# Latent-attention softmax scale folded into q's norm weight, shorter Newton steps, and a reordered start in a two-layer encoder trunk

## What is computed

```python
# rms_norm(x, gain) = x * rsqrt(mean(x*x) + 1e-6) * gain
a_q, a_k, a_v, b_ql, b_kvl, b_kr = split_cols(h @ w_in, (512, 512, 512, 256, 128, 32))
a_q = rope(rms_norm(a_q.reshape(B, S, 8, 64), a_q_norm), pos)          # a_k the same
out_a = differential_attention(..., A_QK_DIM ** -0.5)                  # 4 heads, two softmaxes each
q_b  = (rms_norm(b_ql,  b_q_a_norm)  @ b_w_q_b ).reshape(B, S, 8, 64 + 32)
kv_b = (rms_norm(b_kvl, b_kv_a_norm) @ b_w_kv_b).reshape(B, S, 8, 64 + 64)
q_nope = rms_norm(q_nope, b_q_nope_norm); k_nope = rms_norm(k_nope, b_k_nope_norm)
q_rope = rope(rms_norm(q_rope, b_q_rope_norm), pos); k_rope = rope(rms_norm(b_kr, b_k_rope_norm), pos)
# latent attention, 8 heads, per 128 queries, chunk-causal in chunks of 64 frames
s = (q_nope @ k_nope.T + q_rope @ k_rope.T) * (64 + 32) ** -0.5
p = softmax(where(mask, s, -inf)); out_b = p @ b_v
x = x + concat(out_a, out_b) @ w_out
```

## Time and profile before

| | |
|---|---|
| median of three runs | 1354.26 us |
| profiled run, its own time | 1355.07 us |
| its span | 1353.2 us |
| TensorE busy | 1284.9 us (95%), 6308 matmuls |
| VectorE busy | 617.3 us (46%), 1110 instructions |
| ScalarE busy | 559.3 us (41%), 921 instructions |
| GpSimd busy | 506.2 us (37%), 215 instructions |
| latent units | 89.8 to 211.4 us |
| differential heads | about 211 to 290 us |

### The profile page before, as it was taken

One profiled execution on the slowest core, in us unless ns is written; L12 is line 12 of the kernel. 1 busy time (PEld: TensorE's weight loads), 2 busy tenths in 40 slices (PEclk: granted clock), 3 DMA queues, 4 the chain that ended last, 5 costly groups with the idle time before them and its releaser, 6 DMA issues.

```text
span 1353.2 us, 16953 instructions
## 1 busy us (share of the span) xinstructions
PE 1284.9 (95%) x6308; PEld 1082.6 (80%) x6308; DVE 617.3 (46%) x1110; ACT 559.3 (41%) x921; POOL 506.2 (37%) x215
## 2 busy tenths in 40 slices
PE   8878888999999999999989999998999999999998
PEld 8777887877888888888868888887788888888887
DVE  6579986754222112222248888887332220122211
ACT  5534454654332212223346777775433322122320
POOL 4422311126444434445542222221654454344441
PEclk9888998999999999999989999999999999999999
DMA  5210100012323322233211111110222332222341
GB/s 193 67 63 31 48 32 31 32 41 81 109 93 117 102 78 93 93 105 107 84 64 62 46 46 46 51 57 31 79 94 93 100 118 93 78 93 93 111 131 39
DMA packets 29142, 105.83 MB, mean 78 GB/s; under 512 B 3360, under 2 KB 3616, under 8 KB 29088
## 3 DMA queue, kind: packets, MB, share of 16 engines
q1 hardware_dynamic: 28944, 105.07, 23.5%
q10 hardware_dynamic: 144, 0.02, 0.0%
HBM read 102.98 MB, written 2.10 MB: 78 GB/s over the span
## 4 chain that ended last, share of the span: by engine, by line
PE 68%; DVE 18%; ACT 8%; issue 4%; POOL 1%; DMA 0%; ACTq 0%; DVEq 0%; POOLq 0%
PE bank L338 19%; PE bank L342 19%; PE bank L339 19%; DVE cs_hi L1469 2%; DVE cs_lo L1471 1%; ACT ca L1427 1%; ACT w_hi L314 1%; ACT ca L1425 1%; DVE tiny L1044 1%; ACT cq_hi L1508 1%; DVE pn L1059 1%; PE bank L916 1%; PE bank L1011 1%; PE bank L918 1%; PE bank L920 1%
## 5 line engine op out<-in xcount | busy, mean ns | idle before, releaser
L326 POOL TENSOR_TENSOR w_lo<-wraw,w_hi 128x1024 fp32r<-128x1024 f32 (+4 forms) x180 | 458.3, 2547 | 781.2 <-ACT w_hi L314 781.1
L338 PE MATMUL bank<-h_hi,w_hi 128*128 128x512 f32 x896 | 353.5, 395 | 1.0 <-DVE h_lo L424 1.0
L339 PE MATMUL bank<-h_lo,w_hi 128*128 128x512 f32 x896 | 351.2, 392 | 0.0
L314 ACT ACTIVATE w_hi<-wraw 128x1024 fp32r<-128x1024 f32 (+4 forms) x180 | 197.2, 1096 | 156.7 <-DVE x L631 127.2
L342 PE MATMUL bank<-h_hi,w_lo 128*128 128x512 f32 x896 | 223.6, 392 | 0.0
L338 PEld LDWEIGHTS bank<-h_hi,w_hi 128*128 128x128 f32 x896 | 168.8, 188 | 38.5 <-DVE h_lo L424 1.7
L339 PEld LDWEIGHTS bank<-h_lo,w_hi 128*128 128x128 f32 x896 | 168.9, 189 | 36.2
L342 PEld LDWEIGHTS bank<-h_hi,w_lo 128*128 128x128 f32 x896 | 168.3, 188 | 36.8
L338 PE MATMUL bank<-f_hi,w_hi 128*128 128x512 f32 x352 | 137.7, 391 | 0.0
L339 PE MATMUL bank<-f_lo,w_hi 128*128 128x512 f32 x352 | 137.7, 391 | 0.0
L617 DVE TENSOR_TENSOR fu<-bank,rstd 128x512 f32<-128x512 f32 x44 | 30.4, 691 | 200.3 <-PE bank L342 200.3
(11 more groups left out here) (273 smaller groups left out, 2028.1 us busy)
## 6 DMA issues: line engine op xcount, KB each, us to landing
wraw<-in_w_in SPq DMA_DIRECT2D x120, 512.0 KB, 3.3
wraw<-in_w_down SPq DMA_DIRECT2D x32, 704.0 KB, 4.1
wraw<-in_w_ab SPq DMA_DIRECT2D x20, 512.0 KB, 3.2
x<-in_xt SPq DMA_DIRECT2D x8, 256.0 KB, 5.3
out<-x SPq DMA_DIRECT2D x8, 256.0 KB, 2.1
wraw<-in_w_ab SPq DMA_DIRECT2D x4, 416.0 KB, 5.3
wraw<-in_w_ab SPq DMA_DIRECT2D x2, 384.0 KB, 3.1
wraw<-in_w_ab SPq DMA_DIRECT2D x2, 256.0 KB, 2.8
```

The costliest lines, as they stand in the source:

```text
L314: nc.scalar.activation(whi[:, s, 0:width], wraw[:, s, 0:width], ACT.Copy).then_inc(S("w_hi"), 1)
L326: nc.gpsimd.tensor_tensor(wlo[:, s, 0:width], wraw[:, s, 0:width], whi[:, s, 0:width], ALU.subtract).then_inc(S("w_lo"), 1)
L338: nc.tensor.matmul(out_bank, w, src_hi[kt], start=(kt == 0), stop=False)
L339: nc.tensor.matmul(out_bank, w, src_lo[kt], start=False, stop=False)
```

## The change

It does six things.

- The latent score scale B_SCALE is multiplied into the weight of q's norm (`T_BQ`) once, so scores come scaled; the maximum is then taken negated (`negate=True`) straight into the bias column, L1046 goes, and the exp has scale 1. Newton q0 and q1 likewise give roots with A_SCALE in them, through their means (`T_EQ`), so the step after them (L980) goes.
- A Newton refinement has three instructions instead of four, two of them with a scalar and two tensors; `b_mean_dve` reads eps from a spread column instead of an immediate.
- The probabilities are scaled by a two-tensor multiply with the reciprocal as a spread column, instead of a tensor-scalar one.
- On ScalarE w_hi of chunks 4 and 5 stand ahead of lambda's exp and of the latents' root; GpSimd makes w_lo of chunk 4 before the table tbk. VectorE does lambda after the latents' scaling.
- TensorE's latent transposes stand between the two halves of the first projection. `b_pair(0)` on VectorE stands behind the k/v blocks of the second half.
- In a unit the third projection block stands ahead of the transposes of the probabilities, and all values stand at the end.

```diff
@@ -393,13 +396,11 @@
         dve.wait_ge(S("rs_exp"), r + 1)
-        nc.vector.tensor_tensor(a, m, y, ALU.mult).then_inc(S("rs_step"), 1)
-        dve.wait_ge(S("rs_step"), 3 * r + 1)
+        nc.vector.scalar_tensor_tensor(a, m, -0.5, y, ALU.mult, ALU.mult).then_inc(S("rs_step"), 1)
+        dve.wait_ge(S("rs_step"), 2 * r + 1)
         nc.vector.tensor_tensor(a, a, y, ALU.mult).then_inc(S("rs_step"), 1)
-        dve.wait_ge(S("rs_step"), 3 * r + 2)
-        nc.vector.tensor_scalar(a, a, -0.5, 1.5, ALU.mult, ALU.add).then_inc(S("rs_step"), 1)
-        dve.wait_ge(S("rs_step"), 3 * r + 3)
-        nc.vector.tensor_tensor(tiny[:, at:at + n], a, y, ALU.mult).then_inc(S("rs_root"), 1)
+        dve.wait_ge(S("rs_step"), 2 * r + 2)
+        nc.vector.scalar_tensor_tensor(tiny[:, at:at + n], a, 1.5, y, ALU.add, ALU.mult).then_inc(S("rs_root"), 1)
...
@@ -692,8 +695,9 @@
         dve.wait_ge(S("l_eps"), 1)
-        nc.vector.tensor_scalar(col(T_E, NB), col(T_M + 3 * NB, NB), EPS, None, ALU.mult).then_inc(S("l_eps"), 1)
-        dve.wait_ge(S("l_eps"), 2)
+        for t, scale in ((T_E, EPS), (T_EQ, EPS / A_SCALE ** 2)):
+            nc.vector.tensor_scalar(col(t, NB), col(T_M + 3 * NB, NB), scale, None, ALU.mult).then_inc(S("l_eps"), 1)
+        dve.wait_ge(S("l_eps"), 3)
         dve.wait_ge(S("l_sum"), NB)
...
@@ -857,9 +861,10 @@
         dve.wait_ge(S("bk_sum"), NB * hf + NB)
-        nc.vector.tensor_scalar(col(T_M, 32), col(T_BS + 48 * hf, 32), 1.0 / B_NOPE, EPS, ALU.mult, ALU.add)
-        nc.vector.tensor_scalar(col(T_M + 32, 16), col(T_BS + 48 * hf + 32, 16), 1.0 / B_ROPE, EPS, ALU.mult,
-                                ALU.add).then_inc(S("rs_mean"), 1)
+        nc.vector.scalar_tensor_tensor(col(T_M, 32), col(T_BS + 48 * hf, 32), 1.0 / B_NOPE, spread(col(T_EPS), [P, 32]),
+                                       ALU.mult, ALU.add)
+        nc.vector.scalar_tensor_tensor(col(T_M + 32, 16), col(T_BS + 48 * hf + 32, 16), 1.0 / B_ROPE,
+                                       spread(col(T_EPS), [P, 16]), ALU.mult, ALU.add).then_inc(S("rs_mean"), 1)
...
@@ -968,17 +973,11 @@
         dve.wait_ge(S("pj_sum"), 2 * p + 2)
-        e = spread(col(T_E, NB).rearrange("p (i o) -> p i o", o=1), [P, NB, 4])
+        e, n = ((T_EQ, A_DIM * A_SCALE ** 2), (T_E, A_DIM))[p // 2]
+        e = spread(col(e, NB).rearrange("p (i o) -> p i o", o=1), [P, NB, 4])
         nc.vector.scalar_tensor_tensor(col(T_M, 16).rearrange("p (i j) -> p i j", i=NB),
-                                       col(T_AS + 16 * p, 16).rearrange("p (i j) -> p i j", i=NB), 1.0 / A_DIM, e, ALU.mult,
+                                       col(T_AS + 16 * p, 16).rearrange("p (i j) -> p i j", i=NB), 1.0 / n, e, ALU.mult,
                                        ALU.add).then_inc(S("rs_mean"), 1)
-
-    def q_root_dve(dve, p):
-
-        rs_newton_dve(dve, GROUPS[p], 16, Z_Q + 16 * p)
-        dve.wait_ge(S("rs_root"), ROOT[GROUPS[p]] + 1)
-        nc.vector.tensor_scalar(col(Z_Q + 16 * p, 16), col(Z_Q + 16 * p, 16), A_SCALE, None,
-                                ALU.mult).then_inc(S("a_zq"), 1)
...
@@ -1041,13 +1038,11 @@
         o = bank[0][:].rearrange("p (b n) -> p b n", b=2) if c == 0 else b_score_of(b)
-        nc.vector.reduce_max(col(T_MX + b, n), o, AX).then_inc(S("h_mx"), 1)
-        dve.wait_ge(S("h_mx"), 3 * u + c + 1)
-        nc.vector.tensor_scalar(col(T_NM + b, n), col(T_MX + b, n), -B_SCALE, None, ALU.mult).then_inc(S("h_nm"), 1)
+        nc.vector.tensor_reduce(col(T_NM + b, n), o, AX, ALU.max, negate=True).then_inc(S("h_nm"), 1)
...
         act.wait_ge(S("h_nm"), 3 * u + max(b, 1))
-        nc.scalar.activation(p_of(pn, b), b_score_of(b), ACT.Exp, bias=col(T_NM + b), scale=B_SCALE,
+        nc.scalar.activation(p_of(pn, b), b_score_of(b), ACT.Exp, bias=col(T_NM + b), scale=1.0,
                              accum_out=col(T_L + b)).then_inc(S("h_e"), 1)
...
@@ -1056,7 +1051,8 @@
         for j in range(b, b + n):
-            nc.vector.tensor_scalar(p_of(pn, j), p_of(pn, j), col(T_R + j), None, ALU.mult).then_inc(S("h_p"), 1)
+            nc.vector.tensor_tensor(p_of(pn, j), p_of(pn, j), spread(col(T_R + j), [P, SW[j]]),
+                                    ALU.mult).then_inc(S("h_p"), 1)
...
@@ -1114,14 +1110,14 @@
         nc.scalar.activation(bqhi[0:B_QK, :], bank[TRQ][0:B_QK, :], ACT.Copy,
-                             scale=v(V_BQ, rows=B_QK)).then_inc(S("h_qhi"), 1)
+                             scale=tiny[0:B_QK, T_BQ:T_BQ + 1]).then_inc(S("h_qhi"), 1)
         act.wait_ge(S("h_kt"), u + 1)
...
         dve.wait_ge(S("h_qhi"), u + 1)
-        nc.vector.scalar_tensor_tensor(bqlo[0:B_QK, :], bank[TRQ][0:B_QK, :], v(V_BQ, rows=B_QK), bqhi[0:B_QK, :],
+        nc.vector.scalar_tensor_tensor(bqlo[0:B_QK, :], bank[TRQ][0:B_QK, :], tiny[0:B_QK, T_BQ:T_BQ + 1], bqhi[0:B_QK, :],
                                        ALU.mult, ALU.subtract).then_inc(S("h_qlo"), 1)
...
@@ -1620,12 +1616,11 @@
                                                [P, NB, n]), ALU.mult).then_inc(S("tabs"), 1)
-            for g in range(4):
+            for g in range(5):
                 lo(g)
...
             table(tbk, NB * 2 * A_DIM, 4 * A_DIM + 2 * B_ROPE, 2 * B_ROPE)
-            lo(4)
             lo(5)
...
@@ -1681,13 +1676,13 @@
                     hi_static(act, d // 2)
-            act.wait_ge(S("lam_sum"), 1)
-            nc.scalar.activation(tiny[:, T_LE:T_LE + 2], bank[5][:, 0:2], ACT.Exp).then_inc(S("lam_exp"), 1)
             hi_static(act, 4)
             for i in range(NB):
                 lat_sq_act(act, i)
+            hi_static(act, 5)
             rs_act(act, "lat", 16)
-            hi_static(act, 5)
+            act.wait_ge(S("lam_sum"), 1)
+            nc.scalar.activation(tiny[:, T_LE:T_LE + 2], bank[5][:, 0:2], ACT.Exp).then_inc(S("lam_exp"), 1)
             for i in range(NB):
                 lat_scale_act(act, i)
...
@@ -1840,17 +1835,24 @@
             nc.vector.memset(zeros[:, 0:SEQ].bitcast(F32), 0.0).then_inc(S("zeros"), 1)
+            nc.vector.memset(col(T_EPS), EPS)
             dve.wait_ge(S("vec_in"), 16)
...
                                     ALU.mult)
+            nc.vector.tensor_scalar(tiny[:, T_BQ:T_BQ + 1], v(V_BQ), B_SCALE, None, ALU.mult)
             for d in range(KT):
...
             nc.vector.tensor_copy(ident_r[:], M["ident"])
+            for i in range(NB):
+                lat_sum_dve(dve, i)
+            lat_mean_dve(dve)
+            rs_newton_dve(dve, "lat", 16, Z_LAT)
+            lat_scale_dve(dve)
             dve.wait_ge(S("lam_exp"), 1)
...
@@ -1883,10 +1879,10 @@
                 bq_dve(dve, 1, i)
-            b_pair_dve(dve, 0)
             for i in range(NB):
...
             b_mean_dve(dve, 1)
+            b_pair_dve(dve, 0)
             nc.vector.memset(pthi[:, SEQ + 384:SEQ + 384 + P].bitcast(F32), 0.0)
...
@@ -1918,12 +1914,12 @@
                 if u == 1:
-                    q_root_dve(dve, 0)
+                    rs_newton_dve(dve, "q0", 16, Z_Q)
                 elif u in (3, 5):
...
                     qk_mean_dve(dve, 1)
-                    q_root_dve(dve, 1)
+                    rs_newton_dve(dve, "q1", 16, Z_Q + 16)
                 if u % 2 == 0 and u < 6:
...
@@ -2047,11 +2043,12 @@
             norm_pe(pe, 0, 4)
-            for c in range(2):
-                for i in range(NB):
-                    pj_pe(pe, 0, c, i)
+            for i in range(NB):
+                pj_pe(pe, 0, 0, i)
             pe.wait_ge(S("lam_exp"), 1)
             lat_trans_pe(pe)
+            for i in range(NB):
+                pj_pe(pe, 0, 1, i)
             for i in range(NB):
...
@@ -2077,11 +2074,10 @@
                 pj_pe(pe, p, c, 1)
+                pj_pe(pe, p, c, 2)
                 b_ptrans_pe(pe, u)
-                pj_pe(pe, p, c, 2)
-                b_values_pe(pe, u, 0)
                 pj_pe(pe, p, c, 3)
-                for kb in range(1, NB):
+                for kb in range(NB):
                     b_values_pe(pe, u, kb)
```

22 lines of the change are left out of this document (10 added, 12 removed).

## The result

The changed kernel takes 1356.76 us (median of 20 runs, 1353.27 to 1360.17), the kernel before 1354.62 (20 runs, 1348.30 to 1356.42). The ratio is 1.0027, with a 95% interval of 1.0017 to 1.0037: 0.3% slower, which is within the 0.5% that was called no change. The forecast was 1340.5, range 1331 to 1349, so the time lies outside it. The profiled run of the changed kernel took 1354.36 us, 2.4 less than the median; its span is 1352.5.

What follows compares the result with a forecast made beforehand. TensorE was taken to bound the kernel, with VectorE setting the pace in the eight latent units. Gains of 8.2 (start), 5.0 (units) and 0.6 (heads) made 13.8 us, so 1340.5 us, range 1331 to 1349.

Steps and rivals of the forecast that it cites:

- The start: Up to the first scores: reordered latents and projections gain 5.8 us, moving b_pair(0) 3.0 less 0.6; 8.2 us gained.
- The units: Eight latent units: negated maxima, shorter Newton and TensorE's new order, less dearer probability scaling; 5.0 us gained.
- The heads: Differential heads: three waits for Newton's last step, each step less saving 0.2 us; 0.6 us gained.
- rival B: At the start, the latents' root passes before GpSimd starts its subtraction: -20.3, 1334.0 us; chance 0.22.
- Rival C: Projections' reordering gains nothing, as the q expansion waits as before: only 5.6 us remain, 1348.7; chance 0.15.
- the pair's 2.4 us: Moving b_pair(0) behind the k/v blocks keeps this gain even if the later waits stay where they are.
- rival D: The latent units gain nothing because later transposes eat it: 1346 us; chance 0.12.
- the prediction's estimate of 0.73 us: VectorE's loss a unit from two-tensor probability scaling by the skill's rates; set aside in favour of the trace's rows.
- the 0.45 of the rows: VectorE's loss in us a unit from two-tensor probability scaling, taken from profiled instruction times.
- Rival E: TensorE's clock falls to half in each of the eight units, shown by half clock where none was: 1361 us; chance 0.04.

Runs made afterwards that it cites:

- e1: Changed kernel with tiny's six new columns put into free ones, so buffers behind it stand as before: 1341.57 us, 0.9911 of the kernel before.
- e2: Kernel before with only tiny made six columns longer (543 to 549), moving every buffer behind it by 32 bytes: 1367.48 us, 1.0103 of before.
- e7: e1 with the start in the order of before, b_pair(0) ahead of the k/v blocks too: 1352.37 us, 0.9988 of before.
- e8: As e7, but b_pair(0) stays behind the k/v blocks, where the change put it: 1350.24 us, 0.9974 of before.
- e6: e1 with TensorE's order inside the latent units as before: 1343.60 us, 0.9929 of before.
- e4: e1 with the probabilities scaled by the tensor-scalar form of before: 1341.19 us, 0.9900 of before.
- e5: No kernel's work: matmuls alone, weights and columns at known distances past a multiple of 512 bytes; 512-column pitch 226.7 to 234.4 ns.
- e3: No kernel's work: matmuls alone, buffers at 0, 32, 64 or 96 bytes past a multiple of 128; 512-column pitch 228.9 to 234.3 ns.

## Why the prediction was wrong

**The step that failed** is in the prediction's first paragraph: "No edit touches the work after 330 us except one Newton step in each of two norms". The instructions there are untouched, but the change's first hunk, six more columns in `tiny`, moves every activation by 32 bytes. The term that is missing from the sum is 3552 matmuls by 4.44 ns, 15.8 us; e1 shows 15.2 and e2, which has nothing but it, 13.4. The large products of before all have one layout, so none of their rows could have given its size; but the question should have been asked, and it was not even a rival. With the term taken out (e1) the kernel takes 1341.57 us, where 1340.5 was forecast. The gain is then 12.5 us (10.7 and 11.6 at the two other layouts) against the 13.8 of the sum. That it comes so near is partly luck: the start gave 10.8 us at the median where 8.2 were forecast, and the units and heads together, which e7 has nearly alone, 1.9 us (0.4 to 2.8) where 5.6 were.

**The start** (8.2 forecast): right in its mechanism, near in size. L703 did meet GpSimd, by a margin of 0.19 us where 0.1 was forecast; so rival B did not come. Transposes at 36.36 (36.6), last k/v wait 4.65 (4.5), h_lo 2.88 us (over 2). The 36.36 is two errors that cancel: only two of the three L703 lost a turn (2.25, 0.15 and 1.25 us, where each was to take 1.3 to 2), so the means were ready at 31.9 us and not at 33.2; but two of Newton's steps stood behind tables (0.73 and 0.65 us), so the three took 1.6 us where 0.9 was forecast. The third q block came earlier than forecast, 47.23 against 49, since the second half of the projections ended at 45.0 and not 46.5: the clock was at half for 3.4 us and not longer. First scores are 9.45 us earlier, and the parts by e7 and e8 are 10.8 and 2.1 (8.2 and 2.4). Rival C's time contradicts the prediction's own bound, which kept the pair's 2.4 us: with them it is 1346.3, not 1348.7.

**The units** (5.0 forecast): too high. From first scores to the first differential scores it was 121.6 us before and 119.9 after, but kernels with the same instructions there differ by up to 2.3 us (the table at e6), so this pair alone shows no gain. e7's median allows 1.9 us for units and heads together. What failed is the sum for units 0 to 5, 0.85 us gained: it prices TensorE's new order there at 0.57 us in three units, and against the one profile of e6 the order costs 2.6 to 5.0 us in the six. Part of that is clock: in these six units e6 has 6.8 us at half clock and the five others 13.7 to 17. Units 6 and 7 did gain 0.95 and 2.7 us, about as summed (1.05 and 3.1). Units 0, 2 and 4 gained 1.4, 0.6 and 1.7, but units 1, 3 and 5 lost 1.7, 0.4 and 3.5. The transposes of the probabilities come later, behind the third block, and VectorE's pt_lo, which needs them, and the pair after it do not come earlier: in unit 0 pt_lo starts 8.9 us after the first scores before, 8.8 in the changed kernel and 8.3 in e6, and the pair ends at 17.8, 17.7 and 17.2. So the time that VectorE saved in unit 0 did not reach q of the next head, while TensorE came to its transposes 1.5 us sooner and stood for 3.17 us where it had stood for 1.78. That is the mechanism of rival D, in these units alone. VectorE is busy 107.55 us before and 105.71 after, 1.8 us less; beside that, a sum of 5.0 should have raised a doubt.

The Trainium skill ("VectorE: DVE Perf Modes", Mode 2x_2P) has the two-tensor form make one result a cycle where the tensor-scalar one makes two. The trace agrees with that in the growth: from 256 to 512 columns the two-tensor form goes from 421 to 692 ns and the tensor-scalar one from 350 to 486, 1.06 and 0.53 ns a column. What the prediction's estimate of 0.73 us left out is the part that does not grow: carried back to no columns, an estimate from these numbers, it is 150 ns and 214 ns. The four instructions of a unit thus differ by 0.49 us, as e1 and e4 show, and the 0.45 of the rows was near.

**The heads** (0.6 forecast): each root's wait fell as said, by 0.24 us. From the first differential scores to the FFN the changed kernel gained 2.6 us and e1 1.6. The kernel before had 6.8 us at half clock there, from 225.5, and the changed kernel none; e1 had 3.4. Most of it is not shown to be the change's work: e2, with the instructions of before, was 2.0 us shorter there than the kernel before.

**Rival E** (the clock falls in each unit) did not come: 17 us at half clock in the changed kernel's units, 13.7 before. But the sign that the prediction named is there in small: units 1 and 5 have 3.4 us at half clock each and had none before. They are the two in which TensorE stood over 3 us for q.

## What to carry to other kernels

An edit that changes the size or order of buffers is an edit of every instruction that reads what lies behind them: compute the addresses before and after, and hold the layout fixed when an instruction change is to be judged. Compare traces at the same work, not at the same time; the count of matmuls in a stretch in which TensorE never idles (876, 859, 884) shows a changed pace at once, while busy share and clock show nothing. When one engine sets the pace of a stage, hold a sum over the other engine's waits against that engine's own total (here 5.0 against 1.8 us), and price a reordering also where it makes that engine later, not only where it closes a wait. Judge a stage by several profiles: the units differed by 2.3 us between kernels with the same instructions there.

## What was not expected of the hardware

- The pitch of a 128x128 by 512 fp32r matmul depends on where weights and columns lie relative to each other: 226.7 ns where their addresses differ by a multiple of 256 bytes, 228.9 where the columns lie 64 bytes further (modulo 256), 232.3 to 234.4 at the other multiples of 32 (e5). 3.4% of the pace hangs on it. Why is open: that the two reads meet somewhere in SBUF is a guess that no run tests.
- For 256 columns the order differs: in e5 119.8 ns at differences of 0 and 96, 117.7 at 32, 117.8 at 64. e3, with its differences worked out as above, has 118.6 at 128, 117.3 at 160 and 120.0 at 96. 192 and 224 weren't measured, nor other shapes and types.
- A negated maximum costs no more than a plain one: 678, 546 and 675 ns (512, 384, 512 columns, changed kernel) against 684, 547 and 681 (before).
- Three VectorE instructions of four columns each took 3.50 us beside GpSimd's subtraction and table, 0.31 us without. The middle one passed between the two in 0.15 us, so they do not strictly take turns.
